# Attention on Trainium2: two operations of the compressed branch on GpSimd, and three steps of it issued later

## The reference

```python
s = jnp.einsum('bqgrd,bcgd->bgrqc', qblk, k_cmp, preferred_element_type=jnp.float32)
s = s + bias_tab[rel_bucket(dc)].transpose(2, 3, 0, 1)
p_cmp = masked_softmax(s, dc >= 0)
o_cmp = jnp.einsum('bgrqc,bcgd->bqgrd', p_cmp.astype(v_cmp.dtype), v_cmp)
imp = jnp.einsum('bgrqc,cj->bqgj', p_cmp, cmp_to_slc)
score = jnp.where(forced[None, :, None, :], FORCED_SCORE,
                  jnp.where(valid[None, :, None, :], imp, NEG))
_, sel = lax.top_k(score, n_sel)
# ks, vs: keys and values of the selected blocks of 64
o_slc = jnp.einsum('bgrqnl,bgqnld->bqgrd', p.astype(vs.dtype), vs)
# s, p over a window of 256 keys
o_win = jnp.einsum('bgrqk,bkgd->bqgrd', p.astype(vw.dtype), vw)
return gblk[..., 0:1] * o_cmp + gblk[..., 1:2] * o_slc + gblk[..., 2:3] * o_win
```

## Time and profile before

| | us |
|---|---|
| median of 3 runs | 4293.01 |
| lowest, highest | 4286.76, 4293.42 |
| the profiled execution's own time | 4288.78 |
| its span | 4287.0 |
| PE busy in the span | 4021.7 (94%) |
| DVE busy | 2352.8 (55%) |
| ACT busy | 1632.2 (38%) |
| POOL busy | 409.8 (10%) |

### The profile page before, as it was taken

How to read it: one execution, slowest core, us unless ns; L and a number is a source line. 1 busy time by engine, 2 the same in 40 slices (tenths; PEclk the granted TensorE clock), 3 DMA queues, 4 the chain that set the end, 5 groups by cost and what they waited for, 6 DMA issues and landing times. The chain is left out here.

```text
span 4287.0 us, 63435 instructions
## 1 busy us (share of the span) xinstructions
PE 4021.7 (94%) x23002; PEld 3467.3 (81%) x23002; DVE 2352.8 (55%) x3488; ACT 1632.2 (38%) x2256; POOL 409.8 (10%) x424
## 2 busy tenths in 40 slices
PE   7999999997997799999699999999999999999993
PEld 6888888886886555557599999999999999999983
DVE  5444444445443676643455555555566666666685
ACT  3222222223332676672222333333344434444462
POOL 2000000000231243330100000000000000000001
PEclk9999999998998899999799999999999999999997
DMA  5222232224544411115333343343455545555576
GB/s 214 98 108 98 100 115 108 98 88 168 163 135 142 127 64 41 42 47 187 142 118 127 128 157 138 144 159 137 147 196 191 205 177 201 190 191 203 202 294 257
DMA packets 174438, 626.76 MB, mean 146 GB/s; under 512 B 27184, under 2 KB 71600, under 8 KB 134067
## 3 DMA queue, kind: packets, MB, share of 16 engines
q1 hardware_dynamic: 156836, 566.90, 36.9%
q0 software_dynamic: 12240, 44.57, 2.8%
q10 hardware_dynamic: 5232, 13.63, 0.8%
HBM read 546.24 MB, written 78.80 MB: 146 GB/s over the span
## 5 line engine op out<-in xcount | busy, mean ns | idle before, releaser
L416 PE MATMUL moe_ps<-moe_ht_hi,moe_gu_hi 128*128 128x256 f32 (+4 forms) x3136 | 936.6, 299 | 1.4 <-DVE moe_ht_lo L307 1.4
L418 PE MATMUL moe_ps<-moe_ht_hi,moe_gu_lo 128*128 128x256 f32 (+4 forms) x3136 | 936.1, 298 | 0.0
L417 PE MATMUL moe_ps<-moe_ht_lo,moe_gu_hi 128*128 128x256 f32 (+4 forms) x3136 | 935.6, 298 | 0.0
L228 ACT CAST moe_gu_hi<-moe_gu_raw 128x2048 fp32r<-128x2048 f32 x226 | 430.9, 1907 | 541.8 <-PE moe_ps L418 485.8
L311 DVE TENSOR_TENSOR moe_gu_lo<-moe_gu_raw,moe_gu_hi 128x2048 fp32r<-128x2048 f32 x226 | 517.4, 2289 | 195.0 <-ACT moe_gu_hi L228 194.9
L416 PEld LDWEIGHTS moe_ps<-moe_ht_hi,moe_gu_hi 128*128 128x128 f32 x3136 | 596.2, 190 | 5.2 <-issue 1.7
L417 PEld LDWEIGHTS moe_ps<-moe_ht_lo,moe_gu_hi 128*128 128x128 f32 x3136 | 597.0, 190 | 3.5
L418 PEld LDWEIGHTS moe_ps<-moe_ht_hi,moe_gu_lo 128*128 128x128 f32 x3136 | 596.0, 190 | 0.0
L344 DVE TENSOR_TENSOR moe_yacc<-moe_yacc,moe_ps 128x512 f32<-128x512 f32 x504 | 344.0, 688 | 349.3 <-PE moe_ps L460 348.6
L458 PE MATMUL moe_ps<-moe_wd_hi,moe_hid_hi 128*128 128x512 f32 x1008 | 395.2, 392 | 0.0
L459 PE MATMUL moe_ps<-moe_wd_lo,moe_hid_hi 128*128 128x512 f32 x1008 | 393.4, 390 | 0.0
(11 more groups left out here) (348 smaller groups left out, 6480.8 us busy)
## 6 DMA issues: line engine op xcount, KB each, us to landing
moe_gu_raw<-in_moe_wgu SPq DMA_DIRECT2D x226, 1024.0 KB, 4.9
moe_wd_raw<-in_moe_wd SPq DMA_DIRECT2D x112, 1024.0 KB, 6.7
first_gu<-in_ffn_wgu SPq DMA_DIRECT2D x58, 1024.0 KB, 4.8
ffn_wd_raw<-in_ffn_wd SPq DMA_DIRECT2D x28, 1024.0 KB, 6.8
y_moe<-zeros SPq DMA_DIRECT2D x32, 512.0 KB, 3.0
att_qt<-qt SPq DMA_DIRECT2D x8, 1024.0 KB, 5.0
kt<-kt_rows SPq DMA_DIRECT2D x8, 1024.0 KB, 6.1
shared<-in_w_kvq SPq DMA_DIRECT2D x5, 1024.0 KB, 7.6
```

The costliest lines, as they stand in the source:

```text
L228: act.copy(gu_hi[s][:, :, :, :].rearrange("p a k c -> p (a k c)"), gu_raw[s][:, :]).then_inc(s_gu_hi, 1)
L416: pe.matmul(out[:, 0:W], gu_hi[s][:, half, k, :], ht_hi[:, k, 0:W], start=(k == 0), stop=False)
L417: pe.matmul(out[:, 0:W], gu_hi[s][:, half, k, :], ht_lo[:, k, 0:W], start=False, stop=False)
L418: last = pe.matmul(out[:, 0:W], gu_lo[s][:, half, k, :], ht_hi[:, k, 0:W], start=False, stop=(k == KT - 1))
```

## The change

POOL gets the subtraction of the bound (`center_cmp`, which raises `s_cready` in DVE's place and itself waits for a new semaphore `s_cmin`) and the product that makes the shares (in `scale_cmp`, with a new semaphore `s_shares`, for which it waits itself before it scales `p_cmp` in place). ACT issues `exp_cmp` ahead of group 2's step 3 instead of step 0. On DVE `cmp_scale` stands behind step 4 of group 2 instead of step 1, `block_scores` behind step 0 of group 3 instead of step 4 of group 2, and `select_blocks` behind step 2 of group 3 instead of step 6 of group 2. On POOL `scale_cmp` stands behind the `scale_odd` of the unit's second head instead of in front of it. PE's program is the same.

```diff
--- before.py
+++ after.py
@@ -1417,8 +1417,8 @@
         s_kt, s_keys, s_values = sem("kt"), sem("keys"), sem("values")
         s_scores, s_sread, s_exp, s_scale, s_even_scaled, s_odd_scaled, s_win_scaled = (
             sem(n) for n in ("scores", "sread", "exp", "scale", "even_scaled", "odd_scaled", "win_scaled"))
-        s_cready, s_cexp, s_cscale, s_cscaled, s_sel, s_near = (
-            sem(n) for n in ("cready", "cexp", "cscale", "cscaled", "sel", "near"))
+        s_cmin, s_cready, s_cexp, s_cscale, s_cscaled, s_shares, s_sel, s_near = (
+            sem(n) for n in ("cmin", "cready", "cexp", "cscale", "cscaled", "shares", "sel", "near"))
         s_tr, s_pt, s_pv, s_oevac = (sem(n) for n in ("tr", "pt", "pv", "oevac"))
         s_chain, s_ot_out = sem("chain"), [sem(f"ot_out{s}") for s in range(2)]
         block = ctx.enter_context(nc.Block())
@@ -1496,8 +1496,19 @@
 
         @block.gpsimd
         def _(pool):
+            def per_head(ap):
+                return ap.rearrange("p (h a) -> p h a", a=1).to_broadcast([P, N_HEADS, NBL])
+
+            def center_cmp(i):
+                pc = p_cmp[i % 2]
+                pool.wait_ge(s_cmin, i + 1)
+                pool.tensor_tensor(pc[:, :, :], pc[:, :, :], per_head(c_min[:, :]), ALU.subtract).then_inc(s_cready, 1)
+
             def scale_cmp(i):
                 pool.wait_ge(s_cscale, i + 1)
+                if i >= 2:
+                    pool.tensor_tensor(shares[:, :, :], p_cmp[i % 2][:, :, :], per_head(c_rs[:, :]), ALU.mult).then_inc(s_shares, 1)
+                    pool.wait_ge(s_shares, i - 1)
                 pool.tensor_tensor(p_cmp[i % 2][:, :, :], p_cmp[i % 2][:, :, :],
                                    c_scale[i % 2][:, :].rearrange("p (h a) -> p h a", a=1).to_broadcast([P, N_HEADS, NBL]),
                                    ALU.mult).then_inc(s_cscaled, 1)
@@ -1522,6 +1533,7 @@
                 pool.wait_ge(s_scale, k // 2 + 1)
                 pool.tensor_scalar(p, p, scale[:, k % 8:k % 8 + 1], None, ALU.mult).then_inc(s_odd_scaled, 1)
 
+            center_cmp(0)
             scale_cmp(0)
             for u in range(4 * TILES):
                 i, g = divmod(u, 4)
@@ -1531,11 +1543,13 @@
                 if u:
                     scale_odd(u - 1, 3)
                 if g == 2 and i + 1 < TILES:
-                    scale_cmp(i + 1)
+                    center_cmp(i + 1)
                 if u >= 8:
                     near_bias(u, 2)
                     near_bias(u, 3)
                 scale_odd(u, 1)
+                if g == 2 and i + 1 < TILES:
+                    scale_cmp(i + 1)
                 if u >= 8 and u + 1 < 4 * TILES:
                     near_bias(u + 1, 0)
                     near_bias(u + 1, 1)
@@ -1577,10 +1591,10 @@
             for i in range(TILES):
                 for g in range(N_KV):
                     u = 4 * i + g
-                    if g == 2 and i + 1 < TILES:
-                        exp_cmp(i + 1)
                     for b in range(8):
                         k = 8 * u + b
+                        if g == 2 and b == 3 and i + 1 < TILES:
+                            exp_cmp(i + 1)
                         if b % 2 == 0:
                             p = p_slc[u % 2][:, b // 2, 0:(i + 1) * P]
                         else:
@@ -1639,8 +1653,9 @@
             def cmp_max(i):
                 pc = p_cmp[i % 2]
                 dve.wait_ge(s_sread, cmp_step(i, 3) + 1)
-                chain.step(dve.tensor_reduce(c_min[:, :], pc[:, :, :], AX.X, ALU.min))
-                dve.tensor_tensor(pc[:, :, :], pc[:, :, :], bc(c_min[:, :], NBL), ALU.subtract).then_inc(s_cready, 1)
+                if i:
+                    dve.wait_ge(s_cready, i)
+                dve.tensor_reduce(c_min[:, :], pc[:, :, :], AX.X, ALU.min).then_inc(s_cmin, 1)
 
             def cmp_scale(i):
                 pc = p_cmp[i % 2]
@@ -1651,7 +1666,6 @@
 
                     chain.step(dve.tensor_scalar(c_rs[:, :], c_rs[:, :], valid[:, 0:1], None, ALU.mult))
                 if i >= 2:
-                    chain.step(dve.tensor_tensor(shares[:, :, :], pc[:, :, :], bc(c_rs[:, :], NBL), ALU.mult))
 
                     dve.wait_ge(s_cscaled, i - 1)
                 dve.tensor_tensor(c_scale[i % 2][:, :], c_rs[:, :],
@@ -1659,6 +1673,7 @@
 
             def block_scores(i):
 
+                dve.wait_ge(s_shares, i - 1)
                 chain.step(dve.tensor_reduce(group_p[:, :, :], shares[:, :, :].rearrange("p (g r) c -> p g c r", r=R), AX.X, ALU.add))
                 fours = group_p[:, :, :].rearrange("p g (j c) -> p g j c", c=4)
                 chain.step(dve.tensor_reduce(imp[:, :, :], fours[:, :, :, 0:3], AX.X, ALU.add))
@@ -1733,11 +1748,11 @@
                                 cmp_bias(i + 1, b // 2)
                             if g == 1 and b == 7:
                                 cmp_max(i + 1)
-                            if g == 2 and b == 1:
+                            if g == 2 and b == 4:
                                 cmp_scale(i + 1)
-                            if g == 2 and b == 4 and i + 1 >= 2:
+                            if g == 3 and b == 0 and i + 1 >= 2:
                                 block_scores(i + 1)
-                            if g == 2 and b == 6 and i + 1 >= 2:
+                            if g == 3 and b == 2 and i + 1 >= 2:
                                 select_blocks(i + 1)
             scale_of(8 * 4 * TILES - 2)
             scale_win(8 * 4 * TILES - 1)
```

## The result

The change makes the kernel slower: 4304.0 us in the median (4297.4 to 4307.2, 20 runs) against 4290.4 us (4286.5 to 4298.4, 20 runs) for the kernel before on the same chips. The ratio is 1.0028, with a 95% interval of 1.0021 to 1.0035. The forecast was 4309.

What follows compares the result with a forecast made beforehand. It took PE in the attention part to be bound by waits for DVE and the half clock behind them. Removing 14.6 and 2.4 us, adding 13, 12.5, 7.5 and 2.8 gave net +18.8, so 4309 us, range 4280 to 4328.

Steps and rivals of the forecast that it cites:

- The sign: Whole kernel: slower than before, given chance 0.62, against 0.23 for same and 0.15 for faster.
- the two new waits: Tiles 2 to 6: PE waits about 2.5 us for ACT's copy in group 2, 2.6 for DVE in group 3.
- the clock's term: Tiles 2 to 6: half clock keeps its old price, 22 us, plus 1.5 us a tile, 7.5, for a second stretch.
- `cmp_scale` leaves step 1: Group 2, tiles 2 to 6: PE's waits for DVE before step 4's scores go, 14.6 us gained.
- `block_scores` in group 3: Behind group 3's step 0 PE has no cover: it waits 2.6 us in each of tiles 2 to 6, 13 us.
- ACT behind POOL: Group 2: ACT's exponential waits for POOL's subtraction, so PE's copy comes 2.5 us late in five tiles, 12.5 us lost.
- The sum of tiles 2 to 6: Terms for these tiles: 14.6 us of waits removed; 13 for block scores, 12.5 for ACT, 7.5 for half clock added.
- Start, and tiles 0 and 1: Start costs 0.8 us; tiles 0 and 1 gain 2.4 from the subtraction leaving DVE, lose 2 waiting for POOL.
- POOL holds DVE: DVE's multiplies of steps 3 and 7 meet more POOL operations: charged nothing, at most 1 us a tile.
- The first: Stall only changes place: block_scores takes over cmp_scale's price, ACT's delay is absorbed; 4293 us (4284 to 4301), chance 0.23.
- The second: Clock holds from group 2 to 3 if the block_scores wait stays below about 1.5 us: faster, 4271 us, chance 0.14.
- The third: Two full half-clock stretches per tile and DVE held by POOL: 4324 to 4331 us, chance 0.10.

Runs made afterwards that it cites:

- the one in smaller pieces: The kernel before with all work on DVE, the sum, shares, sum over heads, block sums and choice cut up behind separate late steps of groups 2 and 3: 4264.2 us.
- the kernel with the places alone: The kernel before with its engines, only cmp_scale, block_scores and select_blocks moved to the change's places (GpSimd's scaling behind the second head's scale_odd): 4288.7 us, 0.9996.

## Why the prediction held, and where it did not

The sign, the two new waits and their size were right; the clock's term had the wrong sign, and what the shares and the scaling on POOL do to DVE was put at nothing, where PE waits 1.98 us for it in tile 1 and 1.64 in tile 2. By its steps:

- **`cmp_scale` leaves step 1, 14.6 us.** Right. The wait at group 2's step 4 is gone in tiles 2 to 6, and PE waits for nothing above 0.7 us behind the sum at its new place there. (In tile 0, where DVE sets the pace, it waits 1.05 us.)
- **`block_scores` in group 3, 13 us.** Right: 2.53, 2.68, 2.52, 2.48 and 2.35 us in tiles 2 to 6, 12.6 in sum, and 1.64 more in tile 2, where POOL makes DVE late (below). The kernel that moves the choice alone shows these waits by themselves, 12.8 us. The same wait is there in tile 1, 2.77 us, where the forecast counted none.
- **ACT behind POOL, 12.5 us.** Right in mechanism; 0.80, 2.16, 2.04, 2.51 and 2.58 us, 10.1 in sum. The term took 2.5 for all tiles. In tile 2 POOL's `scale_odd` has 384 columns and takes 1.47 us instead of 2.11, and ACT's scaling ahead of the copies 0.60 instead of 0.81, which is part of the reason. ACT did not catch up in full in any tile.
- **The clock, 7.5 us: mis-sized, with the wrong sign.** The step that failed: the forecast let the half clock come along at its old price and added 1.5 us a tile for the second wait. Two stretches a tile came (one in tile 2), but of 3.4 or 6.8 us each; they sum to 37.5 us, where five stretches before had 47.8. Ten us less at half the rate are up to 5 us of PE's time gained, where 7.5 were charged; the units below show 2.7 of it.
- **The sum of tiles 2 to 6** is seen in the units: groups 2 and 3 together are longer by 1.7, 0.7, 2.4, 1.6 and 1.8 us, 8.2 in all. Summed over these groups PE's idle time grew by 10.9 us, from 20.0 to 30.9, and its busy time fell by 2.7, from 167.6 to 164.9. The forecast's terms for these tiles give 18.4: waits of 10.9 (-14.6 + 13 + 12.5) and 7.5 for the clock. So the gap of 10.2 is the clock's term, 7.5 charged and 2.7 gained. That the waits agree to a tenth is luck: the named ones sum to 9.7 (-14.6 + 12.6 + 10.1, and tile 2's 1.6, which was not charged), and shorter ones make up the rest.
- **Start, and tiles 0 and 1.** The start costs 0.7 us, as said (0.8), but it never reaches the end, nor does what tile 0 gained or lost: in tile 1, group 1, PE waits for the queries in any case, 11.2 us before and 10.7 after. The forecast's terms for the start and tile 0 overlooked this wait. Tiles 0 and 1 together are 1 us longer (93.0 against 92.0); the forecast had 2.4 for the subtraction against 2. More is hidden in that: tile 1's group 2 is 1.6 us shorter, since a wait of 3.41 us is gone, and its group 3 is 4.5 longer, with waits of 1.98 and 2.77 us around its step 0. The forecast counted both stalls from tile 2 on only. Group 1 of tiles 0 and 1 is 1.6 and 1.8 us shorter.
- **POOL holds DVE.** Right as a mechanism; "nothing" as its price was wrong in tiles 1 and 2. DVE's two-column multiply took more than 1 us at two places before and at seven after, up to 1.88 us, its mean went from 212 to 279 ns, and in tile 4 the scaling of the window shares took 2.06 us instead of the usual 0.42, while POOL subtracted:

```profile
1641.77 2.06 DVE L1640 TENSOR_SCALAR att_p_win<-att_p_win,att_scale 128x384 f32<-128x384 f32 x1
```

  These are the us of DVE's relief that do not show in its busy time: 17.1 less 4.7 are 12.4; the multiply grew by 8.5 us in sum (35.7 against 27.2), the scaling of the window by 3.8 (59.7 against 55.9). In tile 4 none of it reaches PE. In tile 1, group 2, it does. There the multiply runs beside POOL's shares, the scaling of the window beside POOL's scaling, DVE comes to the scores of group 3's step 0 only at 1467.69, and PE, done at 1466.18, waits for that read:

```profile
1463.75 1.90 POOL L1510 TENSOR_TENSOR shared<-shared,att_c_rs 128x1024 f32<-128x1024 f32 x1
1463.86 1.80 DVE L1634 TENSOR_TENSOR att_scale<-gates,att_sums 128x2 f32<-128x2 f32 x1
...
1465.70 2.08 DVE L1640 TENSOR_SCALAR att_p_win<-att_p_win,att_scale 128x256 f32<-128x256 f32 x1
1465.72 1.90 POOL L1512 TENSOR_TENSOR shared<-shared,att_c_scale 128x1024 f32<-128x1024 f32 x1
1467.69 0.41 DVE L1721 CUSTOM_DVE_ANT_0 att_p_slc<-win,att_s 128x256 f32<-128x256 f32 x1
...
1468.16 0.51 PE L1786 MATMUL att_s<-kt,att_qt 128*128 128x256 f32 x2 [1.98 <-DVE att_neg_max L1721]
```

  In tile 2 DVE is held in the same way, up to 1522.28, where PE is done at 1521.80; then it waits 0.41 us more for the near bias, which stands behind both operations in POOL's queue and is the last to come. The forecast had looked at tile 4 only, where that work ends in time. This wait at group 3's start in tile 2 is in each kernel that has the shares on POOL (1.17 to 1.89 us), and in none that makes them on DVE, except the one in smaller pieces, which has the sum over the heads in front of that read. The Trainium skill (SBUF — State Buffer, section "SBUF: two separate sides") describes the hold as a lock of a port pair for the length of an instruction; the 2.06 us, which end 0.2 us after the subtraction's end, agree.
- **The rivals.** The first, the stall that only changes its place, is exactly what the kernel with the places alone shows (0.9996); in the changed kernel ACT's delay was not absorbed, which set it apart. The second is what happens when both new waits are taken away: the clock stays at 1.00 in groups 2 and 3, but for 3.4 us in tile 2, and 37 us come off the changed kernel. The third is excluded for the changed kernel: two stretches, yet shorter in sum.
- **The time.** 4309 was forecast, from 18.8 us of terms; the attention lost 10.2 us and the medians 13.6. What is between these two is smaller than what two profiles differ by outside the attention, and isn't traced to a step. That 4304 came so near to 4309 is in part luck: the sum was 8.6 us too high by the attention part, and 5.2 by the medians.

## What to carry to other kernels

A step taken out of one engine's queue gains only what its new place does not charge again: read, for each new place, what the waiting engine still has queued there (here PE had only scores at a unit's first steps, and transposes and values from step 3 on), and move the step to where that is longer than the step. Handing work to an idle engine adds its queue to the path of everyone who waits for the result, and here it also held the engine that was to be relieved; 15 us were lost so, though POOL was idle for 61% of the attention part, and the places alone, with no new engine and better chosen than the change's, brought 27. Where several short stalls each bring half clock, take away all of them before judging one: alone the two gave 18 us each, for waits of 13 and 10 us, and left 27 and 34 us at half clock.

## What the runs showed of the hardware

The time at half clock does not follow from the wait ahead of it. In tile 6 the kernel before waits 2.93 us at group 2's step 4, and the group's mean clock is 0.80. With the choice of blocks late and `cmp_scale` in place, the same wait of the same length is there, with no fall behind it (PE in order of time, and the group's window):

```profile
1799.16 1.09 PE L1771 MATMUL att_s<-kt,att_qt 128*128 128x512 f32 x4 [2.93 <-DVE att_neg_max L1716]
```

```profile
1792.40:1814.20 21.80, 17.68 (x110) 10.68 (x110) 12.89 (x41) 14.99 (x31) 9.85 (x7) 1.00 0.10 31
```

The kernel with the choice moved alone has it a second time, 2.93 us and a clock of 1.00. Behind the waits of 2 to 3.2 us in tiles 2 to 6 of all these kernels the profile shows nothing, 3.4, 6.8 or 10.2 us at half clock; what decides between them is open, and was not tried. Nor do the runs bear out a border at a wait of about 1.5 us, where the forecast's second rival put it: in the kernel with the keys loaded later, waits of 1.29 and 0.67 us in tile 3 have 3.4 us at half clock behind them. As an estimate from these stretches, a forecast should take the price of such a fall as a range from nothing to about 5 us each (half of 10.2), and not as the one value that it has in the kernel at hand.
